# Stick-breaking attention: the diagonal mask products move ahead of the scores, the transposes of a tile behind the value products

## The chip, the cores and the metric

One core of a Trainium2 chip runs the whole program. The metric is device microseconds of one execution, lower is better; the time of a version is the median of its runs.

## What is computed

A two-layer encoder trunk over 1,024 prompt rows and 32 sample rows that carry a cache of 512 past positions. Layer 0 mixes by differential attention, layer 1 by stick-breaking attention; each layer then adds a gated product. The change is in layer 1, whose core is this (16 heads of 64):

```python
z = jnp.einsum('bqhd,bkhd->bhqk', qb.astype(f32), kf) * (B_DH ** -0.5)
valid = k_pos[None, :] < qpb[:, None]
log_keep = jnp.where(valid, jax.nn.log_sigmoid(-z), 0.0)
after = lax.cumsum(log_keep, axis=3, reverse=True) - log_keep
a = jnp.where(valid, jnp.exp(jax.nn.log_sigmoid(z) + after), 0.0)
return jnp.einsum('bhqk,bkhd->bqhd', a, vf)
```

All matmuls keep float32 quality: an operand is split into a high and a low part, and three products (high by high, low by high, high by low) are summed.

## The kernel before

The program runs stages one behind the other: a normalisation with transposes, layer 0 (`diff_layer`, tiles `la_`), its output product and gate (`mix_phase`, `mix_a_`), layer 1 (`stick_layer`, tiles `lb_`), and `mix_b_`. The change touches `stick_layer` alone.

`stick_layer` is a loop of 8 groups of two heads, numbered 0 to 7 here. In a group, `PAIRS` lists 13 pairs of a query chunk c (0 and 1 are 512 prompt rows each, 2 is the sample) and a block b of 128 keys: (0,0) to (0,3), (1,0), the sample (2,0), then (1,1) to (1,7). The loop `for i in range(NP + 1)` of TensorE (PE) makes 14 turns, 0 to 13, and each engine has its own loop with semaphores between them. One turn of PE does, in this order:

- `scores(i)`: six products per pair (L1612), three for each head. A head has 64 features, so these use 64 rows of the array (64*128 in the profile). On a pair on the diagonal (i = 0 to 3 and 9 to 12) the block's upper triangle must be hidden: two products of 128 columns (L1619, one for each head, `unit` by `hide`) add -1e30 there, and release ScalarE (ACT) through the semaphore `z`. On the other pairs the last scores release it.
- `values(i - 2)`: weights by values (L1670), one head in each half of the columns (128*64).
- `after(i - 1)`: two products per head (L1634, 128*128) that add the sums behind each key; they wait for VectorE's (DVE) split of the softplus, `s_high` (L1406) and `s_low` (L1408).
- `column_sums(i - 1)` (L1645), only on pairs with b > 0.
- Work of 12 + 12 products of 384 or 352 columns (L107): the projection of a token tile (`project`, in two halves), of the gate (`gate_project`), or in the last group the start of the output product. Turns 0 to 2 project tiles 6 to 8 of this group, turns 8 to 11 tiles 1 to 4 of the next; turns 6 and 7, and 12 and 13, one half each. Between the two halves stands `turn`: two transposes (L1565, 128 columns each, 32 for the sample's tile) that bring queries and keys of the tile before into the layout for scores.

A pair uses two of the four score banks, in turns; `scores(i)` waits through the semaphore `a` until ACT's `weights` has read the banks of pair i - 2. Turn 1 ends with four transposes of the cached keys (L1718). ACT takes for each pair the size (L1201), the exponential and the logarithm of both heads, then `weights(i - 1)` (L1221). A projected tile goes from PSUM through ACT (`tokens`, L1186 and L1187) to `tok`; from there `turn` reads it, and ACT and DVE split the transposed tile (L1191, L1358) into `qk_high` and `qk_low`; `free_bank` waits for that before a bank takes a new projection.

The order of a turn, in short:

```python
for i in range(NP + 1):
    if i < NP:
        scores(i)
    if i >= 2:
        values(i - 2)
    if i >= 1:
        for s in units(i - 1):
            after(s)
```

Of the kernel before, what the change touches and what calls it, by code (L numbers as in the profile page):

```python
# [27 lines left out]
P = 128  # L28
# [4 lines left out]
NT = SEQ // P  # L33
# [9 lines left out]
QC = 512  # L43
# [943 lines left out]
def stick_layer(nc, top, name, h, w_in, k_past, v_past, k_out, v_out, o_dram, w_out, ident, masks, stage, norm, area, pj):  # L987
# [28 lines left out]
    def span(c, b):  # L1016

        q = max(0, b * P - c * QC)
        return q, QC - q, b >= 4 * c

    with ExitStack() as ctx:
# [523 lines left out]
        def _(pe):  # L1545
# [30 lines left out]
            def body(r, more):  # L1576
# [4 lines left out]
                def scores(i):  # L1581
                    c, b = PAIRS[i]
                    if i >= 2:
                        pe.wait_ge(S["a"], at.nth("a", through(i - 2)))
                    else:
                        pe.wait_ge(S["a"], at.before("a"))
                    if i == 0:
                        pe.wait_ge(S["turned_low"], at.nth("turned_low", 4))
                    if (c, b) == (1, 0):
                        pe.wait_ge(S["turned_low"], at.nth("turned_low", NT))  # L1590
                    if c == 2:
                        pe.wait_ge(S["turned_low"], at.all("turned_low"))
                        pe.wait_ge(S["past_low"], at.all("past_low"))
                        high, low = qk
                        slot = views(units(i)[0])[0]
                        for b in range(SB):
                            for n, (x, y) in enumerate(((0, high), (1, high), (0, low))):
                                for hd in range(2):
                                    f = slice(hd * DH, (hd + 1) * DH)
                                    keys = kpt[x][f, b * P:(b + 1) * P] if b < PB else qk[x][f, 1, SEQ:]  # L1600
                                    last = pe.matmul(slot[:, hd, b * DEC:(b + 1) * DEC], keys, y[f, 0, SEQ:ROWS],
                                                     start=b == 0 and n == 0, stop=n == 2, skip_group_check=True)
                        for hd in range(2):
                            last = pe.matmul(slot[:, hd, PB * DEC:], unit[:, :], hide[:, 0:DEC], **masked)
                        last.then_inc(S["z"], 1)
                        return
                    q = span(c, b)[0]
                    high, low = qk
                    for n, (x, y) in enumerate(((high, high), (low, high), (high, low))):
                        for s in units(i):  # L1610
                            f = slice(UNITS[s][2] * DH, (UNITS[s][2] + 1) * DH)
                            last = pe.matmul(bank(s)[:, q:], x[f, 1, b * P:(b + 1) * P],  # L1612
                                             y[f, 0, c * QC + q:(c + 1) * QC], start=n == 0, stop=n == 2,
                                             skip_group_check=True)
                            if n == 2 and not span(c, b)[2]:
                                last.then_inc(S["z"], 1)
                    if span(c, b)[2]:
                        for s in units(i):
                            pe.matmul(views(s)[0][:, 0:P], unit[:, :], hide[:, :], **masked).then_inc(S["z"], 1)  # L1619

                def after(s):
                    c, b, hd = UNITS[s]
# [73 lines left out]
                        pe.wait_ge(S["g_normed"], at.nth("g_normed", t + 2))  # L1696

                for i in range(NP + 1):
                    if i < NP:
                        scores(i)  # L1700
                    if i >= 2:
                        values(i - 2)
                    if i >= 1:
                        for s in units(i - 1):
                            after(s)
                        if PAIRS[i - 1][1] > 0:
                            column_sums(i - 1)
                    if i < 3:
                        t = TILE_AT[i]
                        free_bank(t)  # L1710
                        project(at, t, 0)
                        turn(at, t - 1)
                        project(at, t, 1)
                    if i == 1:
                        pe.wait_ge(S["past"], at.nth("past", 32))
# [3 lines left out]
                        last.then_inc(S["past_turned"], 1)  # L1719
                    if i in GATE_AT:  # L1720
                        gate_project(GATE_AT[i], 0)
                        if i == 3:
                            turn(at, NT)
                        gate_project(GATE_AT[i], 1)
                    if more:
                        if i == 6:
# [4 lines left out]
                        if 8 <= i <= 11:  # L1731
                            t = TILE_AT[i]
                            free_bank(t)
                            project(ahead, t, 0)
                            turn(ahead, t - 1)
                            project(ahead, t, 1)
                        if i == 12:
                            free_bank(5)
                            project(ahead, 5, 0)
                            turn(ahead, 4)  # L1740
                        if i == 13:
                            project(ahead, 5, 1)
                    elif 7 <= i <= NP:
                        if i == 7:
                            pe.wait_ge(S["g_normed"], at.all("g_normed"))
                            pe.wait_ge(S["out_low"], 1 + 1)
                        begin_output(i - 7)
                values(NP - 1)

            first = Count(table, 0)  # L1750
# [606 lines left out]
```

## Time and profile before

| what | us |
|---|---|
| median of 3 runs | 2026.64 |
| lowest, highest | 2021.52, 2026.65 |
| the profiled execution | 2027.47 |
| its span, first to last instruction | 2025.6 |
| PE busy in the span | 1897.3 |
| mean granted TensorE clock, as a share | 0.975 |

Times in the trace count from the start of the span. A PE row of the timeline gives the start, the length and the instruction with its array shape (rows*columns) and its operand; products are pipelined, so the cost of one is read from the start of it to the start of the next, not from its length. The idle time of an engine stands in brackets with what ended it. PEclk is the clock granted to TensorE as a share of 2.4 GHz.

### The profile page before, as it was taken

The numbers are of one execution on the slowest core, as the hardware profiler recorded it, in microseconds if no ns is written. First come the engines' busy times: TensorE is split into PE (matmuls) and PEld (weight loads), VectorE is DVE, ScalarE is ACT, GpSimd is POOL, SyncE is SP. The second block draws the span as 40 slices with busy tenths as digits, with TensorE's granted clock in tenths as the row PEclk, the third lists the DMA queues.
The fourth block names the chain that finished last, engine by engine and source line by source line (L and its number), as shares of the span: only waits on it lengthen the run. The fifth ranks groups of instructions, "written<-read, shape, count | busy, mean of one in ns | idle before, by whom it ended". The sixth has DMA issues, their size and how long they took to land. (4 is left out here: it accounts for less than half of the span.)

```text
span 2025.6 us, 31736 instructions
## 1 busy us (share of the span) xinstructions
PE 1897.3 (94%) x11429; PEld 1623.9 (80%) x11429; DVE 1122.7 (55%) x2269; ACT 1069.4 (53%) x2556; POOL 387.3 (19%) x597
## 2 busy tenths in 40 slices
PE   4999999999999899997799999999999999889996
PEld 4887878878878699986678787878787778689995
DVE  5556455565564532455165657575657575753555
ACT  5456455454554522454266667566657575732335
POOL 0132222321322000265001111110111011100341
PEclk7999999999999899998899999999999999999999
DMA  4121112111211242211111111111101111243113
GB/s 153 55 66 38 48 51 61 59 49 51 72 38 48 97 122 81 68 63 49 52 48 37 49 38 48 38 48 38 56 30 59 31 55 45 80 125 95 53 52 125
DMA packets 161803, 125.07 MB, mean 62 GB/s; under 512 B 10992, under 2 KB 152624, under 8 KB 161648
## 3 DMA queue, kind: packets, MB, share of 16 engines
q1 hardware_dynamic: 160784, 122.85, 19.8%
q8 instruction: 92, 1.51, 0.3%
q14 instruction: 63, 0.52, 0.1%
q10 hardware_dynamic: 864, 0.20, 0.0%
HBM read 89.49 MB, written 33.52 MB: 61 GB/s over the span
## 5 line engine op out<-in xcount | busy, mean ns | idle before, releaser
L107 PE MATMUL pj<-area,h_high 128*128 128x384 f32 (+1 forms) x2304 | 660.9, 349 | 25.8 <-issue 11.3
L107 PEld LDWEIGHTS pj<-area,h_high 128*128 128x128 f32 (+1 forms) x2304 | 408.2, 181 | 49.2 <-issue 11.4
L107 PE MATMUL pj<-area,h_low 128*128 128x384 f32 (+1 forms) x1152 | 390.8, 339 | 0.0
L107 PEld LDWEIGHTS pj<-area,h_low 128*128 128x128 f32 (+1 forms) x1152 | 210.3, 183 | 8.5
L1530 POOL TENSOR_TENSOR lb_o<-lb_o,lb_keep 128x512 f32<-128x512 f32 (+3 forms) x80 | 77.2, 965 | 603.0 <-ACT lb_keep L1230 596.4
L1375 DVE SCALAR_TENSOR_TENSOR lb_s<-lb_sc,lb_m 128x512 f32<-128x512 f32 (+4 forms) x200 | 109.9, 550 | 73.9 <-ACT lb_m L1211 73.9
L1201 ACT ACTIVATE lb_m<-lb_sc 128x512 f32<-128x512 f32 (+4 forms) x200 | 87.7, 486 | 81.0 <-PE lb_sc L1612 41.0
L455 ACT ACTIVATE la_p<-la_sc,la_nm 128x128 f32<-128x128 f32 (+5 forms) x144 | 105.8, 737 | 33.8 <-DVE la_nm L652 32.9
L1406 DVE CAST lb_s_high<-lb_s 128x512 fp32r<-128x512 f32 (+1 forms) x192 | 105.5, 549 | 25.7 <-DVE lb_s L1375 0.5
L1408 DVE TENSOR_TENSOR lb_s_low<-lb_s,lb_s_high 128x512 fp32r<-128x512 f32 (+1 forms) x192 | 115.5, 601 | 6.6
L650 DVE TENSOR_REDUCE la_mx<-la_sc 128x1 f32<-128x128 f32 (+5 forms) x144 | 107.6, 747 | 2.2
L1425 DVE TENSOR_TENSOR lb_o<-lb_acc,lb_o 128x512 f32<-128x512 f32 (+3 forms) x80 | 42.3, 529 | 112.8 <-PE lb_acc L1670 112.1
L107 PE MATMUL pj<-h_high,area 128*128 128x384 f32 (+1 forms) x384 | 94.4, 331 | 6.0 <-PEq L93 4.7
L1186 ACT ACTIVATE lb_tok<-pj,norm_token 128x128 f32<-128x128 f32 (+1 forms) x72 | 26.4, 367 | 133.2 <-PE pj L107 133.2
L1634 PEld LDWEIGHTS lb_sc<-lb_s_high,lb_tri 128*128 128x128 f32 x192 | 36.4, 189 | 73.6 <-issue 70.1
L1206 ACT ACTIVATE lb_m<-lb_m 128x512 f32<-128x512 f32 (+4 forms) x200 | 93.8, 522 | 0.3
L1211 ACT ACTIVATE lb_m<-lb_m 128x512 f32<-128x512 f32 (+4 forms) x200 | 93.6, 520 | 0.3
L1221 ACT ACTIVATE lb_a<-lb_sc 128x512 f32<-128x512 f32 (+4 forms) x200 | 87.8, 489 | 7.8 <-PE lb_sc L1634 5.9
L107 PE MATMUL mix_b_g<-mix_b_x_high,area 128*128 128x384 f32 (+1 forms) x384 | 91.7, 324 | 0.0
L107 PE MATMUL mix_a_g<-mix_a_x_high,area 128*128 128x384 f32 (+1 forms) x384 | 91.3, 323 | 0.0
L1634 PE MATMUL lb_sc<-lb_s_high,lb_tri 128*128 128x512 f32 (+1 forms) x192 | 76.6, 407 | 13.6 <-DVE lb_s_low L1408 13.5
L757 POOL TENSOR_TENSOR la_ra<-la_tok,cos 128x64 f32<-128x64 f32 (+1 forms) x72 | 23.1, 321 | 335.6 <-ACT la_tok L438 335.6
(307 smaller groups left out, 4491.7 us busy)
## 6 DMA issues: line engine op xcount, KB each, us to landing
stage<-in_a_w_in SPq DMA_DIRECT2D x60, 192.0 KB, 3.5
stage<-in_b_w_in SPq DMA_DIRECT2D x60, 192.0 KB, 3.0
stage<-in_ple_w_gate SPq DMA_DIRECT2D x22, 512.0 KB, 3.8
h_low<-o_t SPq DMA_DIRECT2D x14, 528.0 KB, 6.2
mix_b_xs<-x_mid SPq DMA_DIRECT2D x8, 528.0 KB
lift_xt<-in_x SPq DMA_DIRECT2D x8, 512.0 KB, 4.4
stage<-in_a_w_in SPq DMA_DIRECT2D x16, 256.0 KB, 5.1
out_ak<-la_tok SPq DMA_DIRECT2D x8, 512.0 KB, 3.3
```

What stands on the lines that cost most here:

```text
L107: last = pe.matmul(out, x, y, start=start and n == 0, stop=stop and n == 2, **kw)
L455: act.activation(p[c][u % (3 - c)][0:n, 0:nk], scores_of(u)[:, c, :], ACT.Exp, bias=nm[0:n, u % 2, c:c + 1], accum_out=sums[0:n, u % 2, c: ...
L650: dve.reduce_max(mx[0:n, u % 2, c:c + 1], x[:, c, :], AX.X).then_inc(S["dve_link"], 1)
L1201: act.activation(x, slot, ACT.Abs).then_inc(S["size"], 1)
L1206: act.activation(x, x, ACT.Exp, scale=-1.0).then_inc(S["exp"], 1)
L1211: act.activation(x, x, ACT.Ln, bias=1.0).then_inc(S["log"], 1)
L1221: act.activation(a, slot, ACT.Exp).then_inc(S["a"], 1)
L1375: ins = dve.scalar_tensor_tensor(out=sp, in0=slot, scalar=0.0, in1=x, op0=ALU.max, op1=ALU.add)
L1406: dve.tensor_copy(high, sp).then_inc(S["high"], 1)
L1408: dve.tensor_tensor(low, sp, high.bitcast(F32), ALU.subtract).then_inc(S["low"], 1)
L1530: pool.tensor_tensor(out, out, kept[n % 2][:, q:], ALU.mult).then_inc(S["scaled"], 1)
L1634: last = pe.matmul(slot, tri[:, :], part, **add)
```

## The change

Two things move in PE's order; no instruction is added or dropped, and the other engines' orders are the same.

- The mask products leave `scores` and become `mask(i)`, called at the end of turn i - 1 (and ahead of `scores(0)` for i = 0). They now open the bank (`start=True`) and the scores add to it (`start=not diagonal`); the last scores of a head release `z`. `mask(i)` waits for the same count of `a` as `scores(i)`.
- `turn` leaves the projections and stands behind `values(i - 2)`, ahead of `after(i - 1)`: tiles 5 to 8 of this group in turns 0 to 3, tiles 0 to 4 of the next in turns 8 to 12.

```diff
                             last = pe.matmul(slot[:, hd, PB * DEC:], unit[:, :], hide[:, 0:DEC], **masked)
                         last.then_inc(S["z"], 1)
                         return
-                    q = span(c, b)[0]
+                    q, _, diagonal = span(c, b)
                     high, low = qk
                     for n, (x, y) in enumerate(((high, high), (low, high), (high, low))):
                         for s in units(i):
                             f = slice(UNITS[s][2] * DH, (UNITS[s][2] + 1) * DH)
                             last = pe.matmul(bank(s)[:, q:], x[f, 1, b * P:(b + 1) * P],
-                                             y[f, 0, c * QC + q:(c + 1) * QC], start=n == 0, stop=n == 2,
-                                             skip_group_check=True)
-                            if n == 2 and not span(c, b)[2]:
+                                             y[f, 0, c * QC + q:(c + 1) * QC], start=n == 0 and not diagonal,
+                                             stop=n == 2, skip_group_check=True)
+                            if n == 2:
                                 last.then_inc(S["z"], 1)
-                    if span(c, b)[2]:
-                        for s in units(i):
-                            pe.matmul(views(s)[0][:, 0:P], unit[:, :], hide[:, :], **masked).then_inc(S["z"], 1)
+
+                def mask(i):
+                    if not span(*PAIRS[i][0:2])[2] or PAIRS[i][0] == 2:
+                        return
+                    if i >= 2:
+                        pe.wait_ge(S["a"], at.nth("a", through(i - 2)))
+                    else:
+                        pe.wait_ge(S["a"], at.before("a"))
+                    for s in units(i):
+                        pe.matmul(views(s)[0][:, 0:P], unit[:, :], hide[:, :], start=True, stop=False,
+                                  skip_group_check=True)
 
                 def after(s):
                     c, b, hd = UNITS[s]
@@ -1696,10 +1704,16 @@
...
                         pe.wait_ge(S["g_normed"], at.nth("g_normed", t + 2))
 
                 for i in range(NP + 1):
+                    if i == 0:
+                        mask(0)
                     if i < NP:
                         scores(i)
                     if i >= 2:
                         values(i - 2)
+                    if i < 4:
+                        turn(at, i + 5)
+                    if more and 8 <= i <= 12:
+                        turn(ahead, i - 8)
                     if i >= 1:
                         for s in units(i - 1):
                             after(s)
@@ -1709,7 +1723,6 @@
                         t = TILE_AT[i]
...
-                        turn(at, t - 1)
...
-                        if i == 3:
-                            turn(at, NT)
...
-                            turn(ahead, t - 1)
...
-                            turn(ahead, 4)
...
+                    if i + 1 < NP:
+                        mask(i + 1)
```

PE at the start of a group, from the last value products of the group ahead to the first projection (`lb_acc` takes values, `lb_sc` scores, `lb_hide` is the mask, `pj` the projection or, from `ident`, a transpose). Before:

```order
L1670 MATMUL lb_acc<-lb_a3,lb_tok 64x128
L1670 MATMUL lb_acc<-lb_a0,lb_tok 64x128
L1612 MATMUL lb_sc<-lb_qk_high 128x512 x2
L1612 MATMUL lb_sc<-lb_qk_high,lb_qk_low 128x512 x2
L1612 MATMUL lb_sc<-lb_qk_low,lb_qk_high 128x512 x2
L1619 MATMUL lb_sc<-lb_hide,lb_unit 128x128 x2
L107 MATMUL pj<-area,h_high 128x384
```

Now:

```order
L1678 MATMUL lb_acc<-lb_a3,lb_tok 64x128
L1678 MATMUL lb_acc<-lb_a0,lb_tok 64x128
L1626 MATMUL lb_sc<-lb_hide,lb_unit 128x128 x2
L1612 MATMUL lb_sc<-lb_qk_high 128x512 x2
L1612 MATMUL lb_sc<-lb_qk_high,lb_qk_low 128x512 x2
L1612 MATMUL lb_sc<-lb_qk_low,lb_qk_high 128x512 x2
L1565 MATMUL pj<-ident,lb_tok 128x128 x2
L107 MATMUL pj<-area,h_high 128x384
```

The mask pair has moved between the values and the scores, and the transposes of tile 5 stand where the mask stood.

PE in turn 1, from the end of turn 0's projection to the first products behind softplus. Before:

```order
L107 MATMUL pj<-area,h_high 128x384
L1612 MATMUL lb_sc<-lb_qk_high 128x384 x2
L1612 MATMUL lb_sc<-lb_qk_high,lb_qk_low 128x384 x2
L1612 MATMUL lb_sc<-lb_qk_low,lb_qk_high 128x384 x2
L1619 MATMUL lb_sc<-lb_hide,lb_unit 128x128 x2
L1634 MATMUL lb_sc<-lb_s_high0,lb_tri 128x512
L1634 MATMUL lb_sc<-lb_s_low0,lb_tri 128x512
L1634 MATMUL lb_sc<-lb_s_high1,lb_tri 128x512
L1634 MATMUL lb_sc<-lb_s_low1,lb_tri 128x512
```

Now:

```order
L107 MATMUL pj<-area,h_high 128x384
L1626 MATMUL lb_sc<-lb_hide,lb_unit 128x128 x2
L1612 MATMUL lb_sc<-lb_qk_high 128x384 x2
L1612 MATMUL lb_sc<-lb_qk_high,lb_qk_low 128x384 x2
L1612 MATMUL lb_sc<-lb_qk_low,lb_qk_high 128x384 x2
L1565 MATMUL pj<-ident,lb_tok 128x128 x2
L1642 MATMUL lb_sc<-lb_s_high0,lb_tri 128x512
L1642 MATMUL lb_sc<-lb_s_low0,lb_tri 128x512
L1642 MATMUL lb_sc<-lb_s_high1,lb_tri 128x512
L1642 MATMUL lb_sc<-lb_s_low1,lb_tri 128x512
```

The mask follows the projection directly, and two transposes now stand between the scores and the products that wait for `s_low` (`lb_s_high0` and `lb_s_low0` are head 0, 1 is head 1).

PE in turn 9, a pair on the diagonal with value products. Before:

```order
L107 MATMUL pj<-area,h_high 128x384
L1612 MATMUL lb_sc<-lb_qk_high 128x512 x2
L1612 MATMUL lb_sc<-lb_qk_high,lb_qk_low 128x512 x2
L1612 MATMUL lb_sc<-lb_qk_low,lb_qk_high 128x512 x2
L1619 MATMUL lb_sc<-lb_hide,lb_unit 128x128 x2
L1670 MATMUL lb_acc<-lb_a1,lb_tok 64x512
L1670 MATMUL lb_acc<-lb_a2,lb_tok 64x512
L1634 MATMUL lb_sc<-lb_s_high2,lb_tri 128x512
L1634 MATMUL lb_sc<-lb_s_low2,lb_tri 128x512
```

Now:

```order
L107 MATMUL pj<-area,h_high 128x384
L1626 MATMUL lb_sc<-lb_hide,lb_unit 128x128 x2
L1612 MATMUL lb_sc<-lb_qk_high 128x512 x2
L1612 MATMUL lb_sc<-lb_qk_high,lb_qk_low 128x512 x2
L1612 MATMUL lb_sc<-lb_qk_low,lb_qk_high 128x512 x2
L1678 MATMUL lb_acc<-lb_a1,lb_tok 64x512
L1678 MATMUL lb_acc<-lb_a2,lb_tok 64x512
L1565 MATMUL pj<-ident,lb_tok 128x128 x2
L1642 MATMUL lb_sc<-lb_s_high2,lb_tri 128x512
L1642 MATMUL lb_sc<-lb_s_low2,lb_tri 128x512
```

The scores are now followed by the values at once, and the values by the transposes of tile 1 of the next group.

## Rows read from the trace of the kernel before

**Rows 1.** Page, part 1: busy time, share of the span and instructions of the engines.
```profile
PE 1897.3 (94%) x11429; PEld 1623.9 (80%) x11429; DVE 1122.7 (55%) x2269; ACT 1069.4 (53%) x2556; POOL 387.3 (19%) x597
```
**Rows 2.** Waits of PE, 1004 to 1785 us: us in total, times, longest.
```profile
PE lb_sc L1634 <- DVE lb_s_low L1408: 13.5, 22, 1.2
```
**Rows 3.** Timeline of PE, group 2, turns 8 and 9: start, us, instruction.
```profile
1259.82 0.49 PE L1612 MATMUL lb_sc<-lb_qk_high 64*128 64x512 f32 x2
...
1260.71 1.08 PE L1670 MATMUL lb_acc<-lb_a,lb_tok 128*64 128x512 f32 x4
...
1267.95 0.34 PE L107 MATMUL pj<-area,h_high 128*128 128x384 f32 x1
1268.22 0.49 PE L1612 MATMUL lb_sc<-lb_qk_high 64*128 64x512 f32 x2
...
1269.11 0.44 PE L1619 MATMUL lb_sc<-lb_hide,lb_unit 128*128 128x128 f32 x2
1269.48 1.08 PE L1670 MATMUL lb_acc<-lb_a,lb_tok 128*64 128x512 f32 x4
```
**Rows 4.** Timeline of PE, group 2, turn 13: four column sums of 128 columns.
```profile
1299.71 0.27 PE L1645 MATMUL lb_third<-lb_s_high,lb_half 128*128 128x128 f32 x1
...
1300.16 0.39 PE L107 MATMUL pj<-area,h_high 128*128 128x384 f32 x1
```
**Rows 5.** Page, part 5: the weight loads of the products behind softplus.
```profile
L1634 PEld LDWEIGHTS lb_sc<-lb_s_high,lb_tri 128*128 128x128 f32 x192 | 36.4, 189 | 73.6 <-issue 70.1
```
**Rows 6.** Timeline of PE, group 2, turn 8: two transposes inside a projection.
```profile
1265.63 0.34 PE L107 MATMUL pj<-area,h_high 128*128 128x384 f32 x1
1265.81 0.38 PE L1565 MATMUL pj<-ident,lb_tok 128*128 128x128 f32 x2
...
1266.20 0.34 PE L107 MATMUL pj<-area,h_low 128*128 128x384 f32 x1
```
**Rows 7.** Timeline of PE, group 1, turn 3: the sample's transposes inside the gate projection.
```profile
1133.18 0.32 PE L107 MATMUL pj<-h_high,lb_wg_low 128*128 128x352 f32 x1
1133.34 0.32 PE L107 MATMUL pj<-h_low,lb_wg_high 128*128 128x352 f32 x1
1133.59 0.31 PE L1565 MATMUL pj<-ident,lb_tok 32*128 32x32 f32 x2
...
1134.10 0.33 PE L107 MATMUL pj<-h_high,lb_wg_low 128*128 128x352 f32 x1
```
**Rows 8.** Timelines of PE and ACT, group 2: turns 0 and 1, and turn 8.
```profile
1205.94 0.50 PE L1612 MATMUL lb_sc<-lb_qk_high 64*128 64x512 f32 x2
...
1207.19 1.09 ACT L1201 ACTIVATE lb_m<-lb_sc 128x512 f32<-128x512 f32 x2 [0.70 <-PE lb_sc L1619]
...
1213.88 0.47 PE L1634 MATMUL lb_sc<-lb_s_high,lb_tri 128*128 128x512 f32 x1 [0.53 <-DVE lb_s_low L1408]
...
1260.82 0.60 ACT L1201 ACTIVATE lb_m<-lb_sc 128x512 f32<-128x512 f32 x1
```
**Rows 9.** Timelines of ACT, DVE and PE, group 2, turns 9 and 10.
```profile
1268.68 0.47 ACT L1187 ACTIVATE lb_tok<-pj,norm_token 128x256 f32<-128x256 f32 x1
...
1275.79 0.69 DVE L1408 TENSOR_TENSOR lb_s_low<-lb_s,lb_s_high 128x512 fp32r<-128x512 f32 x1
...
1279.66 0.40 PE L1634 MATMUL lb_sc<-lb_s_high,lb_tri 128*128 128x512 f32 x1
```
**Rows 10.** Timeline of PE, the last group, turn 10.
```profile
1767.14 0.47 PE L1634 MATMUL lb_sc<-lb_s_high,lb_tri 128*128 128x512 f32 x1 [1.18 <-DVE lb_s_low L1408]
```
**Rows 11.** Windows from one group's first scores to the next's: length, busy, PEclk, DMA.
```profile
1107.55:1205.94 98.39, 97.43 (x597) 78.62 (x596) 61.92 (x122) 63.98 (x158) 12.58 (x13) 0.98 0.15 44
1205.94:1302.77 96.83, 95.87 (x596) 77.06 (x595) 61.74 (x122) 64.02 (x158) 12.60 (x13) 1.00 0.15 45
```
**Rows 12.** Windows of PE, 12 us from the sample's scores: length, busy, PEclk, DMA.
```profile
1142.40:1154.40 12.00, 12.00 (x84) 0.86 0.01 2
1240.80:1252.80 12.00, 12.00 (x93) 1.00 0.00 1
```

## The prediction

> **What bounds the kernel now.** I read the page first: TensorE (PE) is busy for 94% of the span, no other engine for more than 55% [rows 1]. So time is won only by making PE's own sequence shorter, or where PE waits. Then the waits of PE in layer 1: little is left there, 13.5 us in 22 waits for VectorE's (DVE) low part of the softplus [rows 2]. Then the timeline of PE, from the start of one product to the start of the next, since that distance and not the busy share shows what a product costs. Here one thing stands out: a step across a change of array shape is longer. From the last projection product to the first scores it is 0.27 us where a step inside the projection is 0.18 [rows 3, 6], and between scores and values the mask pair adds 0.37: from scores to values it is 0.89 us in turn 8, which has no mask, and 1.26 in turn 9 [rows 3]. Four products of the mask's shape (128*128, 128 columns) between others of that shape take 0.45 us, so 0.11 each [rows 4]. Last I read the windows by group: a group is 96.83 us long at full clock and 98.39 in another, where the clock is granted at 0.98 on average [rows 11].
>
> **The mask pairs, turns 2, 3 and 9 to 12.** In turn 9 PE goes from 128*128 (projection) to 64*128 (scores), to 128*128 (mask), to 128*64 (values): three changes. With the mask behind the projection it is two, and the mask stands beside work of its own shape. So the pair costs 2 x 0.11 = 0.22 us there [rows 4] and not 0.37 [rows 3]; the change into the scores (0.27 against 0.18) is paid as before, only after the mask. Gain: 0.15 us a turn. The trace has no mask in the new place, so bounds: nothing gained if the pair costs 0.37 there too, and a loss of 0.23 if each of its weight loads stood bare, 2 x (0.19 + 0.11) = 0.60 [rows 4, 5]. I take 0.22, since the rows of the very shape and neighbourhood (a column-sum pair beside products of the same shape) give it, and the loads beside them also take 0.19 [rows 5] in steps of 0.11 [rows 4]. More than 0.15 can't be gained, as two products of 128 columns stay. Six turns: 0.90 us a group.
>
> A rule speaks against this place. The rows show products 0.11 us apart that each have a load of 0.19 on the same rows of the array [rows 4, 5]. The Trainium skill, TensorE: Matmul & The Clock Gate, Part 3 ("What overlaps and what doesn't"), states that a weight load overlaps with running products only when the row group differs; by it the mask's loads would be hidden behind scores on other rows at best, and stand bare behind the projection. By that rule the sum would be about 8 us longer than before, by the rows it is shorter. The rows decide, and the rule's case is among the rivals with the price above.
>
> The mask's wait for `a` hides nothing: the banks of pair i - 1 are read by ACT's weights early in turn i (L1221 is in ACT's order ahead of the tokens), PE has a whole projection in between, and the same wait stood at the same place ahead of `scores`.
>
> **The start of a group, turns 0 and 1.** Here PE waits. In turn 1 the second head's product stands idle 0.53 us for `s_low` [rows 8], and this chain begins with the release of `z` in turn 0: ScalarE (ACT) begins the size at 1207.19, 1.25 us behind the first scores at 1205.94. Without a mask behind the scores it begins 1.00 behind them, 1259.82 to 1260.82 in turn 8 [rows 3, 8]. But the mask now stands between values and scores, two other shapes, so there it costs the full 0.37 [rows 3]. The chain ends 0.37 - 0.25 = 0.12 us later, and with it PE's wait. On the other side, the transposes of tiles 5 and 6 now run ahead of that wait, not behind it. A pair inside a projection costs 0.21 us: from 1265.63 to 1266.20 it is 0.57, less two steps of 0.18 [rows 6]. The pair of turn 1 stood behind the wait and now fills it (0.21 of 0.53); the pair of turn 0 stays ahead of it. Gain: 0.21 - 0.12 = 0.09 us a group; ends: 0.21 if `z` comes no later, a loss of 0.12 if the pair isn't covered.
>
> **The other transposes.** Two products of 0.11 each cost the same behind the values as in a projection, since the step from values (128*64) to 128*128 is there anyway; no gain in turns 2 and 8 to 12. They must not wait for ACT's tokens: in turn 9 these end at 1268.68 + 0.47 = 1269.15, while the values begin at 1269.48 and last 1 us [rows 3, 9]. The exception is turn 3, the sample's tile of 32 rows: from 1133.34 to 1134.10 it takes 0.76 us, less two steps of 0.16 that is 0.44 [rows 7], because 32*32 stands inside 128*128 and is a change each way. Behind the values one change is there already. Gain between nothing and 0.23 (the cost of a plain pair); I take 0.15.
>
> **The sum.** 0.90 + 0.09 + 0.15 = 1.14 us a group, in groups 0 to 6: 8.0. In the last group PE waits for `s_low` in turns 7 to 12, 1.18 us in turn 10 [rows 10], so its turns 9 to 12 gain nothing and 0.54 is left. Together 8.5; ends 1.9 (masks no cheaper) and 10.1.
>
> **The clock.** In 6 of the 8 groups a piece behind the sample's scores runs at 1.2 GHz (0.86 in a window of 12 us), in two at 2.4, with the same instructions ([rows 12] has one of each; the same windows of the other six groups read 0.86 five times and 1.00 once); such a group is 98.39 - 96.83 = 1.56 us longer [rows 11]. What went before it is the sample's small products, and it comes or not with the instant. Each group will now reach its sample about 1.1 us earlier than the one ahead did, so the count is drawn anew: between none (9.4 less) and eight (3.1 more). I take the middle, four: 3.1 us less.
>
> Total 11.6. The profiled execution took 2027.47 us, 1.9 more than its span, and 0.83 more than the median 2026.64; 2027.47 - 11.6 = 2015.9, and against the median **2015.0**.
>
> **Rivals.**
> - The change doesn't do what it seems to: the mask pair costs 0.37 in the new place too, as part of it may be the entry into the scores. Then 1.9 is left, with the clock's 3.1: 2021.6. For it: no row shows a 128-column product between projection and scores. Chance 0.08.
> - The products behind softplus become the bound in turns 9 to 12 as well, and the shorter sequence only waits. Then 2 to 3 us are left: 2024. Against it: `s_low` ends at 1275.79 + 0.69 = 1276.48 and PE takes it at 1279.66, 3.2 us later [rows 9], and 0.15 a turn doesn't use that up. Chance 0.03.
> - Slower: the mask's weight loads stand bare behind the projection. 0.23 lost in each of six turns, 1.38 a group, less the 0.24 of the two other terms: 7 x 1.14 + 0.2 = 8.2 us, 2035. It decides from 0.15 us of bare load per pair on. Against it: rows 4 and 5 together. Chance 0.04.
> - Slower: the clock falls in further turns, because scores, values and transposes now stand together without dense work between. At 1.56 us each [rows 11], one more in each group gives 2026.6 - 8.5 + 12.5 = 2031, two 2043; from ten more it is slower. Against it: in group 2 the whole 96.83 us run at 1.00, with four transposes of cached keys, scores and values in a row in turn 2 [rows 11]. The Trainium skill, TensorE: Matmul & The Clock Gate, Part 4 (PE-mode transpose), states that transposes don't count as busy for the clock in the same way, which is this case's mechanism; the rows so far show no fall beside one. Chance 0.04.
>
> **How the numbers follow.** The main case has 0.81. Its own range is 2026.6 - 10.1 - 9.4 = 2007 to 2026.6 - 8.5 + 3.1 = 2021. The range 2008 to 2022 holds nearly all of it and part of the first rival, about 0.8. Within 0.3% means within 6.1 us (about what a measurement of this kernel can tell), so faster is below 2020.6: 0.77 of the main case and 0.03 of the first rival, 0.80. Slower: most of the last two, 0.07. The rest, 0.13, is the same.
>
> **What would show it.** In the profile after, in a group with the same clock: from the last projection product to the first scores of turn 9 about 0.49 us (0.27 + 0.22), and from scores to values 0.89, not 1.26. The wait in turn 1 shrinks from 0.53 to about 0.4, and a full-clock group takes about 95.7 us instead of 96.8. PE's count of instructions stays. If the mask step behind the projection reads 0.3 us each, the loads are bare. If new waits of transposes for ACT's tokens or new stretches at 1.2 GHz appear outside the sample's turns, the prediction is wrong in the place named there.

## The result, and the profile after

The changed kernel takes 2005.18 us (median of 4 runs, 2002.79 to 2005.84) against 2024.53 of the kernel before on the same chip (4 runs, 2021.52 to 2026.65): ratio 0.9905, 95% interval 0.9889 to 0.9921. It is faster, as forecast, but by 19.3 us instead of 11.6, and the time lies below the range (2008 to 2022). The profiled execution took 2002.79 us, its span is 2000.9.

The page has the same instructions [rows 1] and 22.8 us less busy time of TensorE (PE), and in layer 1 the waits for the low part of the softplus went from 13.5 us [rows 2] to 11.6. The page, part 1:

```profile
PE 1874.5 (94%) x11429; PEld 1618.4 (81%) x11429; DVE 1122.8 (56%) x2269; ACT 1060.5 (53%) x2556; POOL 387.5 (19%) x597
```

The waits of PE in layer 1 (us in total, times, longest):

```profile
PE lb_sc L1642 <- DVE lb_s_low L1408: 11.6, 20, 1.2
```

The timeline of PE in group 2 of the changed kernel. First turns 0 and 1, then turn 3, then turn 9 (start, us, instruction):

```profile
1196.46 0.44 PE L1626 MATMUL lb_sc<-lb_hide,lb_unit 128*128 128x128 f32 x2
1196.82 0.50 PE L1612 MATMUL lb_sc<-lb_qk_high 64*128 64x512 f32 x2
...
1204.51 0.47 PE L1642 MATMUL lb_sc<-lb_s_high,lb_tri 128*128 128x512 f32 x1 [0.37 <-DVE lb_s_low L1408]
...
1218.89 0.30 PE L1565 MATMUL pj<-ident,lb_tok 32*128 32x32 f32 x2
1219.12 0.39 PE L1642 MATMUL lb_sc<-lb_s_high,lb_tri 128*128 128x256 f32 x1
...
1257.67 0.34 PE L107 MATMUL pj<-area,h_high 128*128 128x384 f32 x1
1257.85 0.33 PE L1626 MATMUL lb_sc<-lb_hide,lb_unit 128*128 128x128 f32 x2
1258.11 0.50 PE L1612 MATMUL lb_sc<-lb_qk_high 64*128 64x512 f32 x2
...
1259.00 1.08 PE L1678 MATMUL lb_acc<-lb_a,lb_tok 128*64 128x512 f32 x4
1260.01 0.44 PE L1565 MATMUL pj<-ident,lb_tok 128*128 128x128 f32 x2
1260.21 0.48 PE L1642 MATMUL lb_sc<-lb_s_high,lb_tri 128*128 128x512 f32 x1
```

In turn 9 the way from the last projection product to the first scores is 0.44 us (1257.67 to 1258.11), where it was 0.27 without a mask [rows 3]: the pair costs 0.17 in its new place. From scores to values it is 0.89, as in a turn without a mask. The transposes behind the values take 0.20 (1260.01 to 1260.21). In turn 0, between values and scores, the mask pair costs 0.36, and the wait in turn 1 shrank from 0.53 [rows 8] to 0.37. ScalarE (ACT) takes up the scores of turn 0 1.00 us behind their start:

```profile
1197.82 1.09 ACT L1201 ACTIVATE lb_m<-lb_sc 128x512 f32<-128x512 f32 x2 [0.81 <-PE lb_sc L1612]
```

The windows by group, from the transposes of the cached keys of one group to those of the next (length, busy of PE, PEld, DVE, ACT, POOL, PEclk, DMA share, GB/s), a group at full clock and the one that is not:

```profile
1209.27:1304.28 95.01, 94.20 (x595) 77.27 (x594) 62.04 (x122) 62.88 (x157) 12.60 (x13) 1.00 0.15 46
1494.27:1591.19 96.92, 95.77 (x596) 78.70 (x595) 62.10 (x122) 62.94 (x157) 12.71 (x13) 0.98 0.15 45
```

A full-clock group went from 96.83 [rows 11] (the same between these marks) to 95.01, by 1.82 us; 1.14 was forecast. The windows of 12 us from the sample's scores, two of the eight (length, busy of PE, PEclk, DMA share, GB/s):

```profile
1420.53:1432.53 12.00, 12.00 (x92) 1.00 0.00 0
1515.54:1527.54 12.00, 12.00 (x84) 0.86 0.00 1
```

One group of eight has the piece at 1.2 GHz behind its sample's scores, where the profile of before has six [rows 12]. Below, such a group is said to have a fall.

One more stretch at 1.2 GHz lies outside the sample's turns, which the prediction named as a sign against itself. It stands in the last group, behind two waits of PE for `s_low` of 0.75 and 1.19 us:

```profile
1743.50:1747.50 4.00, 4.00 (x14) 0.57 0.02 4
```

The kernel before has such a stretch in its last group too, in its second profile (experiment 3; 0.72 from 1742 to 1754 us), and none in its first; it is not the change's alone, and whether the change makes it likelier is not shown.

**Where the time went.** From the first product of turn 0 to the last values layer 1 took 775.1 us in the profile of before and 753.1 after (1009.1 to 1784.2, and 1006.5 to 1759.6); further profiles of the two kernels (below) give 772.1, and 755.4 and 756.0. The means differ by 18.8. Seven groups at 1.82 make 12.7, the last group gains about 1 (it scatters by that much), and falls went from 6 and 4 to 1, 2 and 3, on the mean three fewer at 1.56: 4.7. Together 18.4. The layer ahead and the work behind hold no changed code; what they differ by (turn 0 starts 2.6 us earlier here, 241.4 and 241.3 us behind the last values) is not the change's.

### The profile page after: what moved, and what is told of

It reads as the page before. It is cut to its first block and busy times, and to the rows that moved or that the text cites. A ratio compares the mean times of both kernels' runs of the same rounds, so it can differ in the third digit from the quotient of the medians.

```text
span 2000.9 us, 31736 instructions
## 1 busy us (share of the span) xinstructions
PE 1874.5 (94%) x11429; PEld 1618.4 (81%) x11429; DVE 1122.8 (56%) x2269; ACT 1060.5 (53%) x2556; POOL 387.5 (19%) x597
## 5 line engine op out<-in xcount | busy, mean ns | idle before, releaser
L107 PE MATMUL pj<-area,h_high 128*128 128x384 f32 (+1 forms) x2304 | 649.5, 347 | 26.4 <-issue 11.3
L1408 DVE TENSOR_TENSOR lb_s_low<-lb_s,lb_s_high 128x512 fp32r<-128x512 f32 (+1 forms) x192 | 119.8, 624 | 6.6
L473 ACT ACTIVATE la_wt<-la_third 128x512 f32<-128x512 f32 (+2 forms) x96 | 47.0, 489 | 76.0 <-PE la_third L868 47.4
L633 DVE TENSOR_TENSOR la_qk_low<-pj,la_qk_high 128x256 fp32r<-128x256 f32 (+1 forms) x72 | 28.9, 401 | 101.6 <-ACT la_qk_high L442 101.6
```

The costliest lines, as they stand in the source:

```text
L107: last = pe.matmul(out, x, y, start=start and n == 0, stop=stop and n == 2, **kw)
L473: ins = act.activation(wt[:, k0:k0 + nb, off:off + n], bank, ACT.Copy)
L1408: dve.tensor_tensor(low, sp, high.bitcast(F32), ALU.subtract).then_inc(S["low"], 1)
```

## The experiments

Each is one kernel on the chip. Two questions are asked: why is the group 1.82 us shorter and not 1.14, and what decides whether the clock falls behind the sample's scores.

**1. The two halves apart.** The changed kernel with the transposes back inside the projections (masks only):

```diff
-                    if i < 4:
-                        turn(at, i + 5)
-                    if more and 8 <= i <= 12:
-                        turn(ahead, i - 8)
...
                         project(at, t, 0)
+                        turn(at, t - 1)
                         project(at, t, 1)
...
```

> Only the masks move. Theory A (the terms add up, each read from the profile after): a mask pair saves 0.20 us in each of turns 2, 3 and 9 to 12, and turns 0 and 1 together lose 0.12, so a full-clock group takes 96.83 - 1.08 = 95.75 us and the median falls by 8 to 9 us plus 1.55 for each stretch at 1.2 GHz that is gone. Rival B (the gain needs both moves, since each shape change is shared by them): less than half of it, a group of 96.3 us or more and 2 to 4 us. In turn 9 the two mask products are 0.06 us apart and the first scores start 0.44 us behind the last projection product, as in the changed kernel.

And the kernel before with the transposes moved and the masks left (transposes only), the same lines with the signs turned round:

> Only the transposes move. Theory A: 0.21 us in turns 0 and 1 (they now fill the wait), 0.22 in turn 3 (the sample's tile), 0.03 to 0.05 in each of six other turns: a full-clock group of 96.83 - 0.67 = 96.15 us and 5 us of the median, plus 1.55 for each stretch that is gone. Rival B: next to nothing alone, 96.6 us or more and under 2 us. The prediction's term of no gain for the wide transposes would give 96.4.

Masks only: 2011.37 us (2009.95 to 2013.76), ratio 0.9927 [0.9903, 0.9952]; one fall. Transposes only: 2017.11 (2014.71 to 2020.47), ratio 0.9963 [0.9951, 0.9976]; three falls. A full-clock group of each, by the windows:

```profile
1215.41:1311.08 95.67, 94.68 (x596) 77.44 (x595) 61.73 (x122) 63.55 (x157) 12.57 (x13) 1.00 0.15 45
```

```profile
1218.01:1314.11 96.10, 95.28 (x596) 76.84 (x595) 62.12 (x122) 63.20 (x157) 12.63 (x13) 1.00 0.15 45
```

The masks give 96.83 - 95.67 = 1.16 us a group, the transposes 0.73, together 1.89 against 1.82 for both: the halves add up, and each is worth more than its term (0.90 less the 0.12 of turn 0, and 0.21 + 0.15). Turns 0 and 1 became some 0.1 us longer with the masks alone and 0.22 shorter with the transposes alone, as the terms said (measured from the first product behind the last values of the group ahead to the first transpose of the cached keys: 13.00 and 12.68 us, 12.90 before). The sample's tile gives 0.21 of the 0.73, so 0.30 is left for the other six pairs of transposes, where the prediction has nothing.

**2. What a mask product costs behind a projection.** Each pair three times over (the computation is unchanged, as each pass opens the bank anew):

```diff
-                    for s in units(i):
-                        pe.matmul(views(s)[0][:, 0:P], unit[:, :], hide[:, :], start=True, stop=False,
-                                  skip_group_check=True)
+                    for _ in range(3):
+                        for s in units(i):
+                            pe.matmul(views(s)[0][:, 0:P], unit[:, :], hide[:, :], start=True, stop=False,
+                                      skip_group_check=True)
```

> The changed kernel with each mask pair issued three times in a row (the same values are written three times). Theory P (the pair costs 0.17 us and not 0.22 because its weight loads run ahead behind the longer products of the projection, and the lead is used up after a few): the first two products about 0.06 us apart, the later ones 0.11, so about 0.4 us more in each of the six turns behind dense work. Rival Q (a second product with the same weights is cheap anyway): all six products 0.06 us apart, 0.23 us more a turn. In turn 0, behind the values, both expect the first step at 0.16.

One run: 2035.46 us. The timeline of PE and of its weight loads (PEld) in group 2, turn 9:

```profile
1270.92 0.34 PE L107 MATMUL pj<-area,h_high 128*128 128x384 f32 x1
1271.10 0.78 PE L1627 MATMUL lb_sc<-lb_hide,lb_unit 128*128 128x128 f32 x6
1271.81 0.50 PE L1612 MATMUL lb_sc<-lb_qk_high 64*128 64x512 f32 x2
...
1270.92 0.81 PEld L1627 LDWEIGHTS lb_sc<-lb_hide,lb_unit 128*128 128x128 f32 x6
```

From the first mask product to the scores it is 0.71 us for six and 0.26 for two (1257.85 to 1258.11 above), both with the change of shape at the end. So four further products cost 0.45, or 0.11 each, the price of the column sums [rows 4]; the first two cost 0.17 together, 0.05 less than two at that price. Product by product, the second starts 0.06 us behind the first, and each of the other four 0.11 behind the one ahead of it. The loads begin with the last projection product (1270.92), one product ahead of the one that they serve, and six of 0.19 [rows 5] take 0.81: by these records they overlap the products and each other. That is what theory P said, a lead that the long products leave and the first short ones use up; rival Q (all six 0.06 apart) is out. The full-clock group is 98.10 us, 3.09 longer:

```profile
1221.63:1319.73 98.10, 97.66 (x628) 80.80 (x627) 62.02 (x123) 63.16 (x157) 12.63 (x13) 1.00 0.15 45
```

It has eight pairs; seven at 0.45 make 3.1, and that of turn 1 stands ahead of PE's wait there, which takes it up (turns 0 and 1 together grew by 0.45, not 0.90).

**3. Does the clock's gain belong to the change?** First both kernels again, unchanged.

> The kernel before, unchanged, profiled once more. Theory L (the stretches at 1.2 GHz behind the sample's scores come or not by where in time a group reaches its sample): about 5 or 6 of the 8 groups have one again, not all of them the same groups as in the first profile, full-clock groups again 96.8 us and the others 98.4. Rival F (they belong to fixed groups of the program): exactly groups 0, 1, 3, 4, 6 and 7 again.

> The changed kernel, unchanged, profiled once more. Theory L (a stretch at 1.2 GHz comes by where in time a group reaches its sample; with groups of 95.0 us the landing seldom fits): 0 to 2 of the 8 groups have one behind the sample, in other groups than group 5 if the start differs, and full-clock groups take 95.0 us. Rival R (one in the first profile was luck, the true count is 4 to 5 as in the kernel before): 3 or more.

> The changed kernel once more, to stand beside the next run on one chip. Median 2003 to 2009 us, 0 to 2 groups with a stretch at 1.2 GHz behind the sample's scores, a group at full clock 95.0 us.

Before: 2025.77 us, four falls, in groups 2, 3, 5 and 6 (0, 1, 3, 4, 6 and 7 in the first profile), so no fixed groups. Changed: 2007.94 with two falls (3, 7); then 2007.22 (2005.96 to 2009.83), ratio 0.991 [0.9896, 0.9925], with three (0, 3, 5), one more than expected. Full-clock groups took 96.8 and 95.0 as before.

Then the kernel before, with the products behind softplus of turn 5 put between the key blocks of the sample's scores:

```diff
                         for b in range(SB):
+                            if b == 3:
+                                for s in units(i - 1):
+                                    after(s)
...
-                        for s in units(i - 1):
-                            after(s)
+                        if i != SAMPLE:
+                            for s in units(i - 1):
+                                after(s)
```

> The kernel before, with the two heads' products behind softplus of pair (1,0) put between the third and the fourth key block of the sample's scores, so that the run of small products is cut in two by about 1 us of dense ones. Theory S (the stretches at 1.2 GHz are caused by the unbroken run of the sample's small products): none or at most 2 of the 8 groups still have one; two more shape changes cost 0.2 to 0.4 us a group, so full-clock groups of 97.0 to 97.2 us and a median 5 to 8 us lower. Rival T (landing in time alone decides, whatever runs there): still 5 or 6 stretches, and a median 2 to 3 us higher.

2023.21 us (2020.24 to 2028.47), ratio 0.9986 [0.9974, 0.9999], two falls, a group 0.29 longer: inconclusive. And the changed kernel padded back to the length of a group of before, by ten more products of 384 columns a group:

```diff
                             free_bank(t)
+                            if t <= 2:
+                                for _ in range(5):
+                                    pe.matmul(pj[:, t % 2, 0:NQ], h[0][:, 0, t * P:(t + 1) * P], w[0][:, 0, :],
+                                              start=True, stop=False, skip_group_check=True)
                             project(ahead, t, 0)
```

> The changed kernel with ten more products of 384 columns in a group (five ahead of each of the projections in turns 8 and 9, overwritten by them), so that a full-clock group takes 95.02 + 1.75 = 96.8 us as in the kernel before. Theory L (the count of stretches at 1.2 GHz hangs on the length of a group, hence on landing): 4 to 6 of 8 again, and a median 12 to 14 us (7 groups of 1.75) plus 5 to 8 us above the changed kernel. Rival C (the new order of the instructions avoids them): 0 to 2, and only 12 to 14 us above.

2023.82 us (2020.01 to 2025.75), ratio 0.9985 [0.9975, 0.9994], three falls. A full-clock group, by the windows:

```profile
1024.04:1120.84 96.80, 95.99 (x605) 79.05 (x604) 61.82 (x123) 62.77 (x157) 12.87 (x13) 1.00 0.15 45
```

The padding is 1.79 us in each of seven groups, 12.5, and the median is 15.9 above the 2007.94 of the changed kernel on the same chip, which is one run. Three falls are fewer than the four to six expected, and the changed kernel had three in one profile as well: by the counts it is not shown that the falls come back with the length.

The trace gives more. Within one profile the instants at which the granted clock changes lie whole steps of one grid apart. In the first profile of before the six falls stand 98.99, 194.56, 98.99, 194.56 and 98.98 us apart, while the sample's scores ahead of them start 98.36, 195.22, 98.40, 195.52 and 98.34 us apart: the falls keep to two distances and the starts don't. A fall comes 2.5 to 3.5 us behind the first score product of the sample. Take the start of the sample's scores in each group as a fraction of a step of the grid. In the ten profiles with the sample's own order untouched (before twice, changed three times, experiments 1 and 2, the padded one and the first of experiment 4) there are 80 groups, 29 of them with a fall. All 29 lie between 0.97 and 1 or between 0 and 0.28, and none of the 51 others does (the nearest of these are at 0.28 and 0.96). The split kernel, with another order there, has its two falls at 0.07 and 0.95 and none at 0.16. In the order of the groups, x marks a fall:

| profile | groups 0 to 7 |
|---|---|
| before | 0.15x 0.97x 0.79 0.16x 0.99x 0.80 0.27x 0.08x |
| before, second | 0.45 0.81 0.17x 0.98x 0.80 0.15x 0.07x 0.90 |
| changed | 0.95 0.79 0.63 0.46 0.29 0.12x 0.51 0.35 |
| changed, second | 0.75 0.58 0.43 0.28x 0.57 0.42 0.34 0.17x |
| changed, third | 0.16x 0.45 0.29 0.13x 0.43 0.27x 0.67 0.52 |
| masks only | 0.02x 0.50 0.53 0.55 0.58 0.61 0.75 0.78 |
| transposes only | 0.04x 0.65 0.81 0.96 0.11x 0.72 0.98x 0.58 |
| three mask pairs | 0.33 0.09x 0.30 0.04x 0.24x 0.45 0.30 0.05x |
| mask of turn 0 | 0.76 0.55 0.34 0.12x 0.37 0.16x 0.51 0.28 |
| padded | 0.80 0.16x 0.97x 0.76 0.09x 0.90 0.35 0.68 |

So with the sample's own order the start on the grid tells the falls, and the group's length sets the next start. Before, a group at full clock moves it by +0.37 and one with a fall by +0.82: 0.15, 0.97, 0.79, 0.16, two falls in three groups. Changed, it is -0.16 and +0.29, and a fall throws the next group out of that part. Followed from every possible start, this rule gives about 3.8 falls in eight groups for before (1 to 6), 2.3 for the changed kernel (1 to 3) and 3.9 for the padded one; seen were 6 and 4, then 1, 2 and 3, then 3. These means are worked out; the few profiles agree with them and don't test them.

**4. The masks that still stand ahead of scores between two shapes.** First the pair of turn 0, moved behind the last projection of the group ahead:

```diff
-                    if i == 0:
+                    if i == 0 and r == 0:
                         mask(0)
...
                             project(ahead, 5, 1)
+                            mask(0, ahead)
...
```

> The changed kernel with the first mask of the next group also moved behind a projection: behind the last half of tile 5, ahead of the last value products. By the terms that the profile after shows, the pair costs 0.17 there and not 0.37 between values and scores, so turns 0 and 1 gain 0.20, or up to 0.37 since the release of z comes 0.37 earlier behind the values and PE waits on that chain in turn 1: full-clock groups of 94.65 to 94.82 us, median 1.5 to 2.6 us lower than the changed kernel, plus or minus the stretches at 1.2 GHz. Rival: the wait in turn 1 has another cause than z, then under 0.1 us a group.

Then also the pair of the sample, which no edit had touched so far; it stood behind the sample's scores and now opens their bank behind the gate projection of turn 4:

```diff
-                                                     start=b == 0 and n == 0, stop=n == 2, skip_group_check=True)
-                        for hd in range(2):
-                            last = pe.matmul(slot[:, hd, PB * DEC:], unit[:, :], hide[:, 0:DEC], **masked)
+                                                     start=False, stop=n == 2, skip_group_check=True)
...
+                    if PAIRS[i][0] == 2:
+                        for hd in range(2):
+                            pe.matmul(views(units(i)[0])[0][:, hd, PB * DEC:], unit[:, :], hide[:, 0:DEC], start=True,
+                                      stop=False, skip_group_check=True)
+                        return
...
```

> The changed kernel with the two mask pairs that still stand right ahead of scores moved behind long projection products: the pair of turn 0 (as in e6) and the pair of the sample's scores, which now stands behind the projection of the gate at the end of turn 4. Theory P (a product that follows long products finds its weights loaded; a mask pair costs 0.17 there and 0.32 to 0.37 elsewhere): e6's group of 94.83 us loses another 0.15 to 0.2, so a group at full clock takes 94.63 to 94.70, and the time is 2.5 to 3.5 us under the changed kernel in the same job when both have equally many stretches at 1.2 GHz; each stretch more or less is 1.55 us. Rival (the pair's cost sits in the change of the array's form, which it meets wherever it stands): the group stays at 94.8 and the time within 1.5 us of e6's distance to the changed kernel, none that can be told.

Turn 0 alone: 2007.61 us (2005.86 to 2008.76), ratio 0.9907 [0.9892, 0.9922], no gain in the time that can be told from the changed kernel's 0.9905 and 0.991, though a full-clock group lost 0.18 us. By the rule above a group of that length has 3.1 falls in eight instead of 2.3, and 0.8 at 1.56 would take back most of 8 x 0.18; that is worked out, and the one profile shows two falls. Both: 2002.37 (2000.86 to 2007.73), ratio 0.9889 [0.9871, 0.9906], against 2007.22 of the changed kernel on the same chip (the intervals of the two ratios overlap), and 94.66 a group. The first line is turn 0 alone, the second both:

```profile
1212.56:1307.39 94.83, 94.06 (x595) 77.39 (x594) 62.10 (x122) 62.92 (x157) 12.64 (x13) 1.00 0.16 46
```

```profile
1211.35:1306.01 94.66, 93.90 (x595) 77.43 (x594) 61.81 (x122) 62.94 (x157) 12.70 (x13) 1.00 0.16 46
```

The sample's turn in the timeline of PE, group 2, before and with both moved:

```profile
1240.53 0.32 PE L107 MATMUL pj<-h_low,lb_wg_high 128*128 128x352 f32 x1
1240.77 0.28 PE L1601 MATMUL lb_sc<-lb_qk_high,lb_kpt_high 64*128 64x32 f32 x2
...
1242.55 0.40 PE L1604 MATMUL lb_sc<-lb_hide,lb_unit 128*128 128x32 f32 x2
1242.87 0.44 PE L1670 MATMUL lb_acc<-lb_a,lb_tok 128*64 128x128 f32 x4
```

```profile
1232.39 0.32 PE L107 MATMUL pj<-h_low,lb_wg_high 128*128 128x352 f32 x1
1232.56 0.29 PE L1625 MATMUL lb_sc<-lb_hide,lb_unit 128*128 128x32 f32 x2
1232.78 0.28 PE L1601 MATMUL lb_sc<-lb_qk_high,lb_kpt_high 64*128 64x32 f32 x2
...
1234.55 0.44 PE L1681 MATMUL lb_acc<-lb_a,lb_tok 128*64 128x128 f32 x4
```

From the last projection product to the values it is 2.34 us before and 2.16 now. What was not expected: this profile has no fall at all, though three of its groups start inside the part of the grid that had a fall in all 29 cases (0.03, 0.22 and 0.24).

**5. Is it the sample's mask pair that the clock falls for?** The kernel before with the last edit alone, the pair at the end of turn 4; and the kernel with both pairs moved once more.

```diff
+                    if i + 1 == SAMPLE:
+                        pe.wait_ge(S["a"], at.nth("a", through(SAMPLE - 2)))
+                        for hd in range(2):
+                            pe.matmul(views(units(SAMPLE)[0])[0][:, hd, PB * DEC:], unit[:, :], hide[:, 0:DEC],
+                                      start=True, stop=False, skip_group_check=True)
```

> The kernel before with one edit: the mask pair of the sample's scores stands behind the gate projection at the end of turn 4, ahead of the sample's scores, and not behind them. In ten profiles with the sample's order untouched a group has a stretch at 1.2 GHz where the start of its sample's scores falls in one part (0.97 to 0.28) of the step on which the granted clock changes, and in no other; in the run with all masks moved four groups started in that part and none had the stretch. Both theories: a full-clock group 96.83 less 0.15, 96.65 to 96.70 us. Theory M (the small pair behind the sample's scores is needed for the fall): 0 to 1 stretches in 8 groups, none in the groups that start in that part; with 6 stretches fewer than the profile of before and 1.2 us for the pair the time is 7 to 10 us under the kernel before in the same job, 2015 to 2019. Theory G (the start alone decides): 3 to 6 stretches, in the groups that start in that part, and 0 to 4 us under the kernel before.

> The kernel with all masks moved once more. Theory M: no stretch at 1.2 GHz behind any sample, whatever part of the step the sample's scores start in, 2000 to 2004 us. Theory G: a stretch in each group that starts between 0.97 and 0.28 of the step, which at 94.65 us a group is 2 or 3 of 8, and 2003 to 2008 us. A full-clock group 94.65 us by both.

The first: 2015.66 us (2013.36 to 2017.28), ratio 0.995 [0.9932, 0.9969], 11.2 us under before with two products of 32 columns moved (6 to 14 by the interval; 2.0 of it is 0.25 us in each of eight groups, 0.10 more than expected). There is no fall. The windows of 12 us from the sample's scores, the three groups that start at 0.06, 0.25 and 0.24:

```profile
1041.25:1053.25 12.00, 12.00 (x92) 1.00 0.01 1
...
1427.58:1439.58 12.00, 12.00 (x92) 1.00 0.00 0
...
1717.68:1729.68 12.00, 10.63 (x85) 1.00 0.30 112
```

The second: 2003.25 (one run), no fall behind a sample, with starts at 0.27, 0.99 and 0.00 among the eight. In three profiles with the pair moved, nine groups start where all others fell, and none falls. Theory M holds: in these profiles the clock falls behind a sample only where the pair stands between the sample's scores and the values behind them (2.10 us from the first scores to the values); without it there (1.77 us) the clock stays. Whether it is the pair's time or the change of shape that it brings was not tried. The other runs bear it out in part: the four of the first read a mean granted clock of 0.985 to 0.987, the seven of before beside them 0.975 to 0.983; with both pairs moved it is 0.980 to 0.984 against 0.976 to 0.983 of the changed kernel, which does not tell them apart.

## Why the prediction was right and wrong

**Right.** PE's own sequence was the bound: 94% busy before and after, and each gain there came through to the time. Behind the projection the mask needs one change of shape less; scores to values is 0.89 us, as announced. Turns 0 and 1 gained 0.09, as worked out: from the first product behind the last values of the group ahead to the first transpose of the cached keys it was 12.90 us in group 2 (1205.94 to 1218.84), and is 12.81 (1196.46 to 1209.27). The wait in turn 1 went to 0.37, said was about 0.4. No wait for ACT's tokens appeared ahead of the transposes. The rival with bare loads and the one with masks no cheaper are out by the 0.44 us of turn 9, the one with the softplus as the bound by the group, which lost 1.82 us while the waits for `s_low` went down, and that of falls beside the transposes by the group that reads 1.00 as a whole.

**Wrong: the mask pair.** "More than 0.15 can't be gained, as two products of 128 columns stay" is the step that failed. The pair costs 0.17 and not 0.22 there, since the price of 0.11 came from column sums among other short products, and the first short product behind long ones is cheaper (experiment 2). Six turns gain 0.20 each, 1.2 a group and not 0.90.

**Wrong: the other transposes at nothing.** Behind the values a wide pair costs 0.20 in turn 9, where one inside a projection cost 0.21 [rows 6], and the step behind it is slightly shorter; over the six turns the transposes alone gave 0.30 a group (experiment 1), 0.05 a turn. The sample's tile gains 0.21 where 0.15 was taken: 0.23 (1218.89 to 1219.12) against 0.44 [rows 7], near the upper end of its own bounds.

With these the sum per group is 1.2 + 0.09 + 0.21 + 0.30 = 1.80, against 1.82 measured, and eight groups give 13.7 instead of 8.5. That is 5.2 of the 7.7 us by which the gain was forecast too small. Part of the distance to the forecast time is neither: 2.1 of the 9.8 us from 2015.0 to 2005.18 lie in the kernel before, which had a median of 2026.64 in three runs and 2024.53 in four.

**Wrong: the clock.** Four falls were taken as the middle between none and eight. What fails is the step "the count is drawn anew": the start on the grid follows from the group's length, and 95.0 us is a better length than 96.8, by 3.8 to 2.3 falls worked out and 5 to 2 seen on the mean of two and three profiles. The price of a fall, 1.56 us, was right. That fewer came was called right by luck: the first profile of before, with six, had more than the second, and the middle of none and eight lies below six whatever the change does. The range's lower end rested on the same false bound as the first point: its largest sum was 10.1, and 13.7 came.

## What to carry to other kernels

Price a moved small product by the product that it will follow, not by rows where it stands among its own kind: a pair of 128 columns cost 0.36 us between two other shapes, 0.22 among equals and 0.17 behind long products of its shape. Look where the clock falls before counting instructions: here moving two products of 32 columns a group out from behind a run of small ones gave 11 us in a program of 2,025. Where falls recur in a loop, follow their place on the grid from pass to pass: by the rule found here the length of a pass sets how many come, a shorter pass can have more of them, and a single profile's count (6 and 4, or 1, 2 and 3, of one and the same kernel) is no base for a forecast.

## What the runs showed of the hardware

- Weight loads of 0.19 us on all rows of the array stand beside products on the same rows: six take 0.81 us in experiment 2, and a product 0.11. The first of them starts with the last projection product, at 1270.92. That is against the rule cited in the prediction (the Trainium skill, TensorE: Matmul & The Clock Gate, Part 3).
- The same instructions see the clock fall or not by their start on a grid that lies elsewhere in each execution (29 of 29 inside one part, 0 of 51 outside). The Trainium skill, TensorE: Matmul & The Clock Gate, Part 1, states that the monitor of the clock runs freely and isn't set anew by a kernel's start; the traces agree: the sample's first scores start 1044.03 us into the span of the first profile of before and 1044.08 into that with masks only, and lie at 0.15 and 0.02 of a step.
- The granted clock falls while PE is busy without a gap: the window of the group with the fall reads 12.00 us busy of 12.00 at 0.86. What PE did in the 2.5 to 3.5 us before a fall were 30 score products of 32 columns, the mask pair, four value products and the first products behind softplus; the same with the pair moved ahead of the scores kept 1.00 in all 24 groups.
